# A state-update stage reordered: VectorE updates a state before it makes the low part of the weights, inverse roots sit in four partition groups, and two state loads move one head ahead

## What is computed

```
def _retention(q, k, v, s0, chunk):
    ...
        state = state * s_dec[None, :, None, None] + jnp.einsum('bjhd,bjhe->bhde', kc * k_dec[None, :, :, None], vc)
...
ha = (B, T, N_A_GROUPS * A_HEADS, A_HEAD_DIM)
qa = (_partial_rope(_rmsnorm(qa.reshape(ha), a_q_norm), pos) * A_SCALE).reshape(g5)
ka = _partial_rope(_rmsnorm(ka.reshape(ha), a_k_norm), pos).reshape(g5)
```

## Time and profile before

| | us |
|---|---|
| median of 3 runs | 940.2 (939.92 to 940.85) |
| the profiled execution, its own time | 939.62 |
| its span, first to last instruction | 937.6 |
| busy in it: PE, DVE, ACT, POOL | 918.5, 596.2, 490.0, 219.3 |

### The profile page before, as it was taken

One profiled execution on the slowest core, in us unless ns is written; L12 is line 12 of the kernel. 1 busy time (PEld: TensorE's weight loads), 2 busy tenths in 40 slices (PEclk: granted clock), 3 DMA queues, 4 the chain that ended last, 5 costly groups with the idle time before them and its releaser, 6 DMA issues.

```text
span 937.6 us, 19594 instructions
## 1 busy us (share of the span) xinstructions
PE 918.5 (98%) x8007; PEld 873.2 (93%) x8007; DVE 596.2 (64%) x851; ACT 490.0 (52%) x758; POOL 219.3 (23%) x233
## 2 busy tenths in 40 slices
PE   9999999999999999989998999999999999999998
PEld 8999999999999888878898999789999999999998
DVE  6666655569965577687778653445547766666443
ACT  6444434464544766756766455336766744443342
POOL 0433330006700000068872103000001033333000
PEclk9999999999999999999999999989999999999999
DMA  9988878999888677889988687839999899998971
GB/s 356 396 301 306 306 258 304 357 379 376 311 294 278 227 270 277 281 319 363 319 301 267 226 285 249 282 126 323 350 330 339 302 337 383 337 365 298 337 230 51
DMA packets 62569, 281.17 MB, mean 300 GB/s; under 512 B 8177, under 2 KB 9329, under 8 KB 60881
## 3 DMA queue, kind: packets, MB, share of 16 engines
q10 hardware_dynamic: 39024, 131.61, 42.0%
q1 hardware_dynamic: 23456, 148.31, 41.8%
HBM read 256.64 MB, written 111.32 MB: 392 GB/s over the span
## 4 chain that ended last, share of the span: by engine, by line
PE 80%; DVE 10%; ACT 4%; issue 3%; DMA 1%; POOL 1%; SPq 0%; ACTq 0%; DVEq 0%; POOLq 0%
PE acc L410 17%; PE acc L412 16%; PE acc L411 16%; PE att L410 6%; PE att L411 6%; PE att L412 6%; DVE wl L390 2%; ACT wh L384 2%; DVE state L986 2%; PE att L800 2%; PE aux L995 1%; PE aux L1105 1%; PE att L1046 1%; PE att L1135 1%; PE att L750 1%
## 5 line engine op out<-in xcount | busy, mean ns | idle before, releaser
L390 DVE TENSOR_TENSOR wl<-raw,wh 128x1024 fp32r<-128x1024 f32 (+2 forms) x280 | 333.9, 1194 | 254.8 <-ACT wh L384 249.4
L384 ACT ACTIVATE wh<-raw 128x1024 fp32r<-128x1024 f32 (+2 forms) x280 | 277.2, 993 | 206.4 <-PE acc L412 147.2
L410 PE MATMUL acc<-hh,wh 128*128 128x264 f32 x496 | 148.1, 299 | 0.1
L412 PE MATMUL acc<-hh,wl 128*128 128x264 f32 x496 | 140.7, 284 | 0.0
L411 PE MATMUL acc<-hl,wh 128*128 128x264 f32 x496 | 140.7, 284 | 0.0
L410 PE MATMUL acc<-xh,wh 128*128 128x264 f32 x416 | 118.7, 285 | 1.1 <-DVE wl L390 1.1
L410 PE MATMUL att<-xh,wh 128*128 128x264 f32 x416 | 118.5, 285 | 0.0
L411 PE MATMUL att<-xl,wh 128*128 128x264 f32 x416 | 117.9, 283 | 0.0
L411 PE MATMUL acc<-xl,wh 128*128 128x264 f32 x416 | 117.9, 283 | 0.0
L412 PE MATMUL att<-xh,wl 128*128 128x264 f32 x416 | 117.8, 283 | 0.0
L412 PE MATMUL acc<-xh,wl 128*128 128x264 f32 x416 | 117.8, 283 | 0.0
(11 more groups left out here) (254 smaller groups left out, 1917.9 us busy)
## 6 DMA issues: line engine op xcount, KB each, us to landing
raw<-w ACTq DMA_DIRECT2D x207, 512.0 KB, 6.7
state<-state_in SPq DMA_DIRECT2D x32, 512.0 KB, 7.8
state_out<-state SPq DMA_DIRECT2D x32, 512.0 KB, 5.4
raw<-w ACTq DMA_DIRECT2D x32, 384.0 KB, 5.7
kv<-cache SPq DMA_DIRECT2D x48, 256.0 KB, 4.7
raw<-w ACTq DMA_DIRECT2D x32, 320.0 KB, 5.3
raw<-w SPq DMA_DIRECT2D x9, 512.0 KB, 8.8
kv_out<-cache SPq DMA_DIRECT2D x3, 960.0 KB, 6.7
```

Source lines behind the costliest of these rows:

```text
L384: nc.scalar.activation(wh[n % HI_RING][:, 0:slot_size(n)], raw[n % RAW_RING][:, 0:slot_size(n)], ACT.Copy).then_inc(hi_done, 1)
L390: nc.vector.tensor_tensor(wl[n % RAW_RING][:, 0:slot_size(n)], raw[n % RAW_RING][:, 0:slot_size(n)], wh[n % HI_RING][:, 0:slot_size(n)].bi ...
L410: nc.tensor.matmul(out, w_hi, xh, start=first, stop=False)
L412: return nc.tensor.matmul(out, w_lo, xh, start=False, stop=last)
```

## The change

It has four parts. In DVE's queue the update of the next slot's state goes ahead of this slot's low part, where before a slot's state stood at the head of the slot (behind the low part of the slot before). `STATE_SLOT` begins at slot 1 in place of 2 and its states stand 31/23 of a slot apart in place of 30/23; the last two remain at 30 and 32. The query/key inverse root is computed in the four partition groups in which the sums lie (128 partitions by 64 in place of 32 by 256), with one square root in place of four, and ACT then copies the four groups into rows; the second root stands ahead of the high part of slot 25, its split ahead of that of slot 26, and the samples' sum of squares moves from slot 25 to slot 26. The state buffers are used in another order, so that SP issues the loads of states 8 and 9 behind the third head's store, and that of state 10 once that store has landed.

```diff
+        qk_rinv4 = at("qk_rinv4", 90368, [AE])
...
-            for e in range(4):
-                ins = nc.scalar.activation(qk_rinv[0:32, e * AE:(e + 1) * AE], qk_ms(which, e), ACT.Sqrt, bias=eps[0:32],
-                                           scale=1.0 / AE)
-            ins.then_inc(qk_rms_done, 1)
+            nc.scalar.activation(qk_rinv4[:], bank5[:, which * S:which * S + AE], ACT.Sqrt, bias=eps,
+                                 scale=1.0 / AE).then_inc(qk_rms_done, 1)
...
-            nc.vector.reciprocal(qk_rinv[0:32], qk_rinv[0:32]).then_inc(qk_rinv_done, 1)
+            nc.vector.reciprocal(qk_rinv4[:], qk_rinv4[:]).then_inc(qk_rinv_done, 1)
...
+            for e in range(4):
+                nc.scalar.activation(qk_rinv[0:32, e * AE:(e + 1) * AE], qk_rinv4[32 * e:32 * e + 32], ACT.Copy).then_inc(qk_rows, 1)
+            act.wait_ge(qk_rows, 4 * which + 4)
             nc.scalar.activation(qk_rhl[0:32], qk_rinv[0:32], ACT.Copy).then_inc(qk_rhi, 1)
...
-            pe.wait_ge(qk_rms_done, 1)
+            pe.wait_ge(qk_rms_done, 2)
...
-        STATE_AT = [8 + s % 4 if s < 8 else s % 8 if s < 24 else (s - 24) % 5 for s in range(STATES)]
+        STATE_RING = (0, 2, 4, 1, 3, 5, 6, 7)
+        STATE_AT = [8 + s % 4 if s < 8 else STATE_RING[s % 8 if s < 24 else (s - 24) % 5] for s in range(STATES)]
...
-        STATE_SLOT = {2 + (s - EARLY_STATES) * 30 // 23: s for s in range(EARLY_STATES, STATES)}
+        STATE_SLOT = {1 + (s - EARLY_STATES) * 31 // 23: s for s in range(EARLY_STATES, STATES)}
...
                 if h == RH - 1:
-                    sp.wait_ge(snew_psum, RH)
-                    for n in range(8, 11):
-                        sp_state_load(sp, n)
+                    sp.wait_ge(ret_stored, 16 * (RH - 1))
+                    sp_state_load(sp, 10)
                 sp_state_store(sp, 2 * h + 1)
                 ret_store(sp, h)
                 if h < 2:
                     sp_state_load(sp, 2 * h + 4)
+                if h == 2:
+                    for n in (8, 9):
+                        sp_state_load(sp, n)
...
                 state_pick(2 * AT + t)
                 state_scale(2 * AT + t)
+                if t == 1:
+                    act_qk_rms(act, 1)
+                if t == 2:
+                    act_qk_rhi(act, 1)
...
                 act_v_tile(act, p_v, t)
-                if t == 1:
-                    act_qk_rms(act, 1)
+                if t == 2:
                     act_qk_samples(act)
-                if t == 2:
-                    act_qk_rhi(act, 1)
...
-                if s in STATE_SLOT:
-                    dve_state(dve, STATE_SLOT[s])
...
-                dve_ahead(dve, q, j)
                 if s in (AT + 4, 2 * AT + 3):
                     dve_qk_rlo(dve, s // (2 * AT))
+                if s + 1 in STATE_SLOT:
+                    dve_state(dve, STATE_SLOT[s + 1])
+                dve_ahead(dve, q, j)
...
-                if s == 2 * AT + 1:
-                    steps[5].append(lambda: pe_qk_samples(pe))
+                if s == 2 * AT + 2:
+                    steps[1].append(lambda: pe_qk_samples(pe))
```

More of the change, by code:

```diff
@@ L320, in trunk_step @@
             sem("qk_sq_done"), sem("qk_sq_s"), sem("qk_ms_psum"), sem("qk_rms_done"), sem("qk_rinv_done"))
-        qk_rhi, qk_rlo, qks_ms, qks_rms, qks_rinv, qks_done = (
-            sem("qk_rhi"), sem("qk_rlo"), sem("qks_ms"), sem("qks_rms"), sem("qks_rinv"), sem("qks_done"))
+        qk_rows, qk_rhi, qk_rlo, qks_ms, qks_rms, qks_rinv, qks_done = (
+            sem("qk_rows"), sem("qk_rhi"), sem("qk_rlo"), sem("qks_ms"), sem("qks_rms"), sem("qks_rinv"), sem("qks_done"))
         qk_swapped, qk_sin, qk_cos, qk_turned, qk_spread, qk_done = (
```

## The result

| | us |
|---|---|
| changed kernel, median of 4 runs | 929.7 (927.96 to 931.06) |
| kernel before, median of 4 runs beside it | 940.06 (939.77 to 940.85) |
| ratio | 0.9885, 95% interval 0.9872 to 0.9899 |
| the profiled execution of the changed kernel | 930.28, span 928.5 |

The kernel is faster by 10.4 us in these medians, where 8.6 were forecast. 929.7 lies 0.3 us under the lower edge of the range, 930.0. Five further runs (the first experiment) gave 930.5 as their median, and all nine 930.4, just inside it.

A forecast was written before the change was run, and what follows sets the result against it. PE was taken as the bound, busy for 918.5 of 937.6 us. The terms -7.6 - 1.8 - 0.7 + 1.5 = -8.6 us took the profiled 939.6 to 931.0; plus 0.6 gave 931.6 us, range 930.0 to 936.8.

The forecast's parts named there:

- the rivals: Late state loads 936.6 (0.13); half the waits stay 935.4 (0.08); DVE chain bounds 943.6 (0.05); no change 940.2 (0.04).
- DVE does the state first, -7.6: From 395 to 560 us, PE's nine waits for DVE's state updates at L971 and an unnamed 0.2 go: -7.6 us.
- L697, -0.7: PE's wait for ACT at L697 goes, as ACT's L681 comes earlier: -0.7 us (bounds 0 and -0.7).
- L920, -1.8: PE's wait at L920 for the low part of the second inverse root goes: -1.8 us.
- The walk from the end of slot 24: Forecast times for the second inverse root: square root 2.5, low part ready 12.8, PE at L920 13.2 us.
- The new wait, +1.5: At slot 1, PE's L971 of state 8 waits for ACT's selector copy: +1.5 us (bounds 0 and 2.6).
- State loads, 0.: Earlier loads of states 8 and 9, and state 13's landing, cost PE nothing: 0; upper end +5.0 us.
- a sign of being wrong: ACT's L980 idle behind a DMA, listed among what would show the forecast wrong.
- the rule that I weighed against the trace: About 358 GB/s HBM per core: the 420 to 444 us stretch could win nothing, the sum 1.2 us less.
- I charge 0.18 us on top of each wait (0.23 in that pair): Extra cost of each PE wait beyond its listed length; the nine L971 waits then make 7.4 us.
- The pair of slots: Slots ending at 428.37 and 432.37, same work: 4.57 us with a 0.34 us L971 wait, 4.00 without.
- the median is 0.6 above it: Whole kernel: the median lies 0.6 us above the profiled execution, turning 931.0 into the forecast 931.6 us.

The follow-up runs named there:

- the first experiment: The changed kernel run again, unchanged: median 930.51 us (928.19 to 932.35, 5 runs), ratio 0.9901 to the kernel before.

## Why the mechanism was right, and which steps of the number failed

**The mechanism** was as forecast, and none of the rivals occurred. The number was not: 931.6 us were forecast and 929.7 measured, outside the range. Each step, by its number:

- *DVE does the state first, -7.6.* Right in kind. The spacings in the trace before give 7.2 us for the nine named waits and 0.38 for two rows too close behind their matmul to be named (0.16 at 396.30, which I had at 0.2, and 0.22 at 477.88, which I had missed): 7.6 ahead of the rows. Behind all eleven the next matmul followed after 0.30 or 0.31 in place of 0.23: 0.85 more. The part was worth 8.46. The run with DVE's order alone shows that this part alone removes the nine named waits.
- *L697, -0.7*: 0.74 (0.53 for the named wait, 0.21 for one too short to be named), also by DVE's order alone.
- *L920, -1.8*: 1.79, and 0.10 behind it. The walk from the end of slot 24 (489.46) held at every station: square root at 2.3 (walked 2.5), reciprocal 6.3 to 6.8 (6.4 to 6.9), split done at 8.4 (8.8), the samples' reciprocal 10.6 to 11.9 (11.0 to 12.3), low part at 12.4 (12.8), PE at 13.2 (13.2). The reciprocal took 0.54 (taken as 0.5), a copy 0.25 (taken as 0.31).
- *The new wait, +1.5*: 1.46, and 0.08 behind it. The row stands at 395.20, released by the copy at 394.75. I had walked both 0.5 earlier, and the whole execution is 0.5 later at this point (387.23 against 386.73 at the first mark), so the distance was right.
- *State loads, 0.* ACT waited 0.5 us once for one (state 13, scaled at 416.70, walked at 415.9), PE never. I had named such a wait of ACT as a sign of being wrong; it came, and cost PE nothing. All 32 landed after 4.7, 8.7 and 14.6 us (least, median, most) in place of 3.4, 7.8 and 14.1. The stretch from 420 to 444 us carries 418 GB/s where it carried 363, and PE is busy in all 24.00 of it. So the rule that I weighed against the trace did not hold. (The Trainium skill, page "SBUF — State Buffer", section "SBUF: two separate sides", gives about 358 GB/s of HBM for a core; these windows disagree.) In the same way the estimate of 0.15 us for a copy, by the page "ScalarE: Activation LUTs" of the Trainium skill, section "What ACT_TABLE_LOAD costs", was low: a copy took 0.25, and the four in a row 1.09, or 0.27 each. Without the overlap of 93 ns, the figures of the same section of the Trainium skill give an estimate of 0.24 us; the length agrees, and only the overlap does not show in this row.

**The step of the sum that failed is the size of the first term**, "I charge 0.18 us on top of each wait (0.23 in that pair)". The pair of slots gave 0.23, and the reading of two overlapping matmuls gave 0.16; I took the lower side. The spacings give 0.16 ahead of the row and 0.08 behind it, 0.24 together, so the pair was right: 0.5 us over nine waits. Another 0.3 is the row at 477.88, a term that I had put at nothing because the list of waits does not name it. It starts 0.34 behind the matmul ahead of it, and the next one 0.31 behind the row:

```profile
477.54 0.28 PE L412 MATMUL att<-hh,wl 128*128 128x264 f32 x1
477.88 0.47 PE L971 MATMUL aux<-vr_hl,picked 128*128 128x512 f32 x1
478.19 0.28 PE L410 MATMUL att<-hh,wh 128*128 128x264 f32 x1
```

With both, the terms are -8.46 - 0.74 - 1.79 + 1.54 = -9.45, against 9.58 measured in the stage; 0.10 of the rest is the loss behind L920. The first term thus explains 0.86 of the 0.98 us by which -8.6 was short there.

**The step that took the forecast out of its range is "the median is 0.6 above it".** I had set the sum 0.6 above the profiled execution, because the median of before was. In the changed kernel the median of its first four runs lay 0.6 below the profiled execution. Of the 1.9 us between 931.6 and 929.7, 0.7 is the sum's (931.0 against 930.28) and 1.2 is this offset turned round. That part is the luck of the draw: the time of one and the same program moves by about 2 us, and over nine runs the median is 930.4. The range's lower edge was too near as well: it was the forecast less the whole new wait (940.2 - 10.1), and left nothing for this scatter or for a first term that is larger than its rows say.

## What to carry to other kernels

An engine that stands at work needed three slots later, with work needed at once queued behind it, costs waits though it is idle for a third of the time: turn the two, and check that the later one has slack. Cost a wait by the spacing of the starts of the rows around it, on both sides, not by its named length: a wait of 0.3 us cost almost twice that. When a first stall goes, the next part is worth more than alone (the roots: 0.9 us alone, 1.8 behind the order), while a part that only moves work earlier can lose (the slot: 0.9 us), so try each part on top of the others.

## What the runs showed that I had not expected

- In every profiled execution TensorE runs at its lower level (0.50, 1.2 GHz) for some microseconds near 610 to 628 us, with PE busy throughout. The windows give a loss of 3.4 us before (2.0 + 1.4) and 3.4 after (0.8 + 2.0 + 0.6), and 5.1 in the second profile of the changed kernel and in that with spread matmuls. Of these executions the first two have a mean clock of 0.996 and the other two of 0.994, as such losses make of 930 us. The changed kernel's medians at 0.994, 0.996 and 0.998 are 931.2, 930.4 and 928.1 us. So this loss seems to make much of the scatter, more than anything in the stage that was changed; no execution at 0.998 was profiled, so that step is not shown.
- A single wait of 2.1 us was followed by a stretch at half clock that cost 1.7 us more. Before, the 1.6 us wait at the same place had no such stretch. The kernel with this wait had three of its six runs at 0.994 and three at 0.996, so it probably does not occur in each; that was not tried.
- 418 GB/s with a DMA share of 1.03 in a window of 24 us went along with an undisturbed PE.
